# The indexer's keys and weights as one projection output, the keys' second copy by a transfer

## The reference, cut to what matters

```python
proj = h @ w_in                                   # (512, 1024) @ (1024, 3656)
(aq, ak, av, bq, bk, bv, cq, ck, cv, iq, ik, iw) = split(proj)
# iq: 8 heads x 64, ik: 64 (one key for all heads), iw: 8 weights
iw = iw * 8 ** -0.5
logits = einsum('bqhd,bkd->bqhk', iq, ik) * 64 ** -0.5
score = einsum('bqhk,bqh->bqk', relu(logits), iw)
score = where(key <= query, score, NEG)
_, idx = top_k(score, 128)
# attention of kind c over the keys idx only
```

## Time and profile before

| | |
|---|---|
| median of 3 runs | 2800.58 us (2800.39 to 2800.69) |
| the profiled execution, its own time | 2799.84 us |
| its span | 2797.8 us |
| TensorE busy | 2741.3 us, 98% |
| VectorE, ScalarE, POOL busy | 1171.8, 1029.3, 1110.1 us |
| mean granted TensorE clock | 0.995 of full speed |
| loads of packs | 456 of 512 KB, 3.6 us to landing (median) |

### The profile page before, as it was taken

One profiled execution on the slowest core, in us unless ns is written; L12 is line 12 of the kernel. 1 busy time (PEld: TensorE's weight loads), 2 busy tenths in 40 slices (PEclk: granted clock), 3 DMA queues, 4 the chain that ended last, 5 costly groups with the idle time before them and its releaser, 6 DMA issues.

```text
span 2797.8 us, 35422 instructions
## 1 busy us (share of the span) xinstructions
PE 2741.3 (98%) x12394; PEld 2174.0 (78%) x12394; DVE 1171.8 (42%) x1912; ACT 1029.3 (37%) x1571; POOL 1110.1 (40%) x473
## 2 busy tenths in 40 slices
PE   8999999999999999989989999999999999999998
PEld 6777777888887888846878888888888764788887
DVE  4886534654434224258873222122221266422212
ACT  4455533444333232352223222232222467422221
POOL 3334433444454444512214444544444410544443
PEclk9999999999999999999999999999999999999999
DMA  5333322333332333322203333333233310333332
GB/s 169 113 99 116 104 76 62 98 97 93 109 106 89 99 91 99 119 75 67 65 24 104 98 97 98 105 98 101 94 97 105 98 39 1 107 96 97 97 103 86
DMA packets 78106, 258.18 MB, mean 92 GB/s; under 512 B 8951, under 2 KB 14583, under 8 KB 77768
## 3 DMA queue, kind: packets, MB, share of 16 engines
q1 hardware_dynamic: 70848, 243.30, 28.4%
q10 hardware_dynamic: 7176, 13.78, 1.5%
HBM read 251.02 MB, written 6.03 MB: 92 GB/s over the span
## 4 chain that ended last, share of the span: by engine, by line
PE 93%; DVE 5%; ACT 1%; issue 1%; ACTq 0%; DVEq 0%
PE ps L765 27%; PE ps L767 27%; PE ps L766 27%; PE ps L1356 1%; PE ps L1338 1%; PE ps L1325 1%; PE ps L1329 1%; PE ps L985 1%; PE ps L1120 1%; PE ps L1052 1%; PE ps L1062 1%; PE ps L986 0%; PE ps L987 0%; PE ps L970 0%; PE ps L887 0%
## 5 line engine op out<-in xcount | busy, mean ns | idle before, releaser
L718 POOL TENSOR_TENSOR wlo<-raw,whi 128x1024 fp32r<-128x1024 f32 x449 | 1097.8, 2448 | 1640.4 <-ACT whi L1425 1615.6
L765 PE MATMUL ps<-lin_hi,whi 128*128 128x512 f32 x2208 | 867.8, 393 | 6.6 <-DVE waves_tmp L2445 6.6
L767 PE MATMUL ps<-lin_hi,wlo 128*128 128x512 f32 x2208 | 860.2, 390 | 0.0
L766 PE MATMUL ps<-lin_lo,whi 128*128 128x512 f32 x2208 | 860.2, 390 | 0.0
L1425 ACT ACTIVATE whi<-raw 128x1024 fp32r<-128x1024 f32 x452 | 473.3, 1053 | 513.8 <-PE ps L767 446.6
L765 PEld LDWEIGHTS ps<-lin_hi,whi 128*128 128x128 f32 x2208 | 415.1, 188 | 99.7 <-DVE waves_tmp L2445 7.4
L766 PEld LDWEIGHTS ps<-lin_lo,whi 128*128 128x128 f32 x2208 | 415.2, 188 | 88.1 <-issue 2.9
L767 PEld LDWEIGHTS ps<-lin_hi,wlo 128*128 128x128 f32 x2208 | 415.1, 188 | 87.0
L765 PE MATMUL ps<-act_hi,whi 128*128 128x512 f32 x858 | 334.0, 389 | 0.0
L767 PE MATMUL ps<-act_hi,wlo 128*128 128x512 f32 x858 | 333.8, 389 | 0.0
L766 PE MATMUL ps<-act_lo,whi 128*128 128x512 f32 x858 | 333.8, 389 | 0.0
(11 more groups left out here) (374 smaller groups left out, 2702.7 us busy)
## 6 DMA issues: line engine op xcount, KB each, us to landing
raw<-in_packs SPq DMA_DIRECT2D x456, 512.0 KB, 3.6
table<-bias_scratch ACTq DMA_DIRECT2D x12, 256.0 KB, 2.9
bias_scratch<-biasrow ACTq DMA_DIRECT2D x16, 160.0 KB
x<-in_x_t SPq DMA_DIRECT2D x4, 512.0 KB, 8.0
out_t<-x SPq DMA_DIRECT2D x16, 128.0 KB, 1.8
bias_scratch<-biasrow ACTq DMA_DIRECT2D x4, 320.0 KB
mem<-in_mem_t ACTq DMA_DIRECT2D x1, 1024.0 KB, 7.7
pool_count<-in_pool_count ACTq DMA_DIRECT2D x1, 1024.0 KB, 4.8
```

The source lines that it names most:

```text
L718: pool.tensor_tensor(wlo[:, n % 4, :], raw[:, n % 2, :], whi[:, n % 4, :].bitcast(F32), ALU.subtract).then_inc(low_split, 1)
L765: pe.matmul(target, wh, hi[:, k, :], start=(chunk0 + at == 0), stop=False)
L766: pe.matmul(target, wh, lo[:, k, :], start=False, stop=False)
L767: mm = pe.matmul(target, wl, hi[:, k, :], start=False, stop=(chunk0 + at == total - 1))
```

## The change

The keys and the weights are made by one output. Its pack is put together by the load: for each of the 8 chunks the first 64 columns of the keys' pack and the first 64 of the weights' pack, so that rows 0 to 63 of the output are the keys and rows 64 to 71 the weights. The second copy of the keys, for the logits of the other half of the rows, is made by a transfer within the on-chip memory, issued by ScalarE in slot 4, into the tile that held the weights; TensorE waits for it before the first index logits. The mixer has 29 outputs, and three padding packs. The keys' output is fourth, IQ + 3 fifth. The constants that place side work by slots are one less, except `BIAS_A_AT`; step 0 of ScalarE splits two packs, and TensorE passes two padding packs in it. The identity's transfer counts into the semaphore of the bias's inputs, which frees a semaphore for the copy.

```diff
-N_MIXER = 30
+MIXER_TILES = 30
+N_MIXER = MIXER_TILES - 1
+KEYS_AGAIN = IW
-MIX_ORDER = [IQ, IQ + 1, IQ + 2, IQ + 3, IK, IW] + [t + h for h in range(4) for t in (AQ, AK, AV)] + \
-    [...] + [30, 31]
+MIX_ORDER = [IQ, IQ + 1, IQ + 2, IK, IQ + 3] + [t + h for h in range(4) for t in (AQ, AK, AV)] + \
+    [...] + [30, 31, 31]
...
-BIAS_A_AT, BIAS_B_AT = 2, 6
-IDX_AT = 6
-A_FROM = 10
+BIAS_A_AT, BIAS_B_AT = 2, 5
+IDX_AT = 5
+A_FROM = 9
...
@@ sync, load
+            if n == behind(IK) - 1 and i is None:
+                sp.dma_start(raw[:, n % 2, :].rearrange("p (k s c) -> p k s c", k=DC, s=2),
+                             A["packs"][IK:IW + 1].rearrange("s p (k c) -> p k s c", c=P)[:, :, :, 0:64]).then_inc(raw_arrived[n % 2], 16)
+                return
@@ tensor, index_weights
-            pe.wait_ge(outs_done, behind(IW))
+            pe.wait_ge(outs_done, behind(IQ + 3))
...
-                mm = pe.transpose(ps[:, 2, t * 8:(t + 1) * 8], proj[0:8, IW, t * P:(t + 1) * P], ident[0:8, 0:8])
+                mm = pe.transpose(ps[:, 2, t * 8:(t + 1) * 8], proj[64:72, IK, t * P:(t + 1) * P], ident[64:72, 64:72])
@@ tensor, index_logits
                 pe.wait_ge(root_ready, 1)
+                pe.wait_ge(keys_copied, 16)
...
-                          proj[r:r + 64, IK, 0:(qt + 1) * P], start=True, stop=True).then_inc(idx_logits, 1)
+                          proj[r:r + 64, (IK, KEYS_AGAIN)[side], 0:(qt + 1) * P], start=True, stop=True).then_inc(idx_logits, 1)
@@ tensor, steps
-            if s < 2:
-                pe.wait_ge(low_split, N_MIXER + s + 1)
-                pe.wait_ge(packs_used, N_MIXER + s)
+            for n in ((29, 30), (31,))[s] if s < 2 else ():
+                pe.wait_ge(low_split, n + 1)
+                pe.wait_ge(packs_used, n)
                 pe.sem_inc(packs_used, 1)
@@ scalar, between
+            if n == behind(IK):
+                act.wait_ge(outs_done, behind(IK))
+                act.dma_start(proj[64:P, KEYS_AGAIN, :], proj[0:64, IK, :]).then_inc(keys_copied, 16)
@@ scalar, steps
+            if s == 0:
+                split_high(N_MIXER + AHEAD)
             if s < PAIR_STEPS + KV_FROM:
-                split_high(N_MIXER + AHEAD + s)
+                split_high(N_MIXER + AHEAD + 1 + s)
@@ vector, slots
-                              ALU.mult).then_inc(outs_done, 1 if n < N_MIXER - 1 else 3)
+                              ALU.mult).then_inc(outs_done, 1 if n < N_MIXER - 1 else 33 - N_MIXER)
```

More of the change, by code:

```diff
@@ L93 @@
 AQ, AK, BQ, BK, CQ, CK, IQ, IK, IW, AV, BV, CV = 0, 4, 8, 10, 12, 14, 16, 20, 21, 22, 26, 28
-N_MIXER = 30
-MIX_ORDER = [IQ, IQ + 1, IQ + 2, IQ + 3, IK, IW] + [t + h for h in range(4) for t in (AQ, AK, AV)] + \
-    [t + h for q, k, v in ((BQ, BK, BV), (CQ, CK, CV)) for h in range(2) for t in (q, k, v)] + [30, 31]
+MIXER_TILES = 30
+N_MIXER = MIXER_TILES - 1
+KEYS_AGAIN = IW
+MIX_ORDER = [IQ, IQ + 1, IQ + 2, IK, IQ + 3] + [t + h for h in range(4) for t in (AQ, AK, AV)] + \
+    [t + h for q, k, v in ((BQ, BK, BV), (CQ, CK, CV)) for h in range(2) for t in (q, k, v)] + [30, 31, 31]
 V_TILES = [AV, AV + 1, AV + 2, AV + 3, BV, BV + 1, CV, CV + 1]
@@ L115 @@
 APART = 8
-BIAS_A_AT, BIAS_B_AT = 2, 6
-IDX_AT = 6
-A_FROM = 10
+BIAS_A_AT, BIAS_B_AT = 2, 5
+IDX_AT = 5
+A_FROM = 9
 TURN_AT, PRODUCT_AT, SUM_AT, SUM_READ_AT, ROOT_AT, SCALE_AT = A_FROM + 2, A_FROM + 6, A_FROM + 7, A_FROM + 8, A_FROM + 9, A_FROM + 10
-V_AT = (12, 13, 15, 19, 23, 24, 28, STEPS_AT + 2)
-MEM_AT = 13
-TOP_FROM, TOP_TO = 8, N_MIXER - 1
+V_AT = (11, 12, 14, 18, 22, 23, 27, STEPS_AT + 2)
+MEM_AT = 12
+TOP_FROM, TOP_TO = 7, N_MIXER - 1
 def top_rounds(n):
@@ L261, in build_program @@
     put, m1 = region(big_at)
-    proj = put("proj", [P, N_MIXER, T])
+    proj = put("proj", [P, MIXER_TILES, T])
     o_hi_at = m1["at"]
@@ L443, in build_program @@
     cols_arrived = sem("cols_arrived")
-    ident_arrived = sem("ident_arrived")
+    keys_copied = sem("keys_copied")
     rel_arrived = sem("rel_arrived")
@@ L840, in bias_rows @@
         def bias_rows():
-            pe.wait_ge(rel_arrived, 16 * 2)
+            pe.wait_ge(rel_arrived, 16 * 3)
             pe.wait_ge(rel_apart, 1)
@@ L953, in _ @@
                 bias_rows()
-                pe.wait_ge(ident_arrived, 16)
             between(n)
@@ L1552, in _ @@
         act.dma_start(relb[:, :], A["rel_bias"]).then_inc(rel_arrived, 16)
-        act.dma_start(ident[:, :], A["ident"]).then_inc(ident_arrived, 16)
+        act.dma_start(ident[:, :], A["ident"]).then_inc(rel_arrived, 16)
         act.wait_ge(mask_cleared, 1)
@@ L2160, in _ @@
         order(dve.memset(relb_apart[:, :], 0.0))
-        dve.wait_ge(rel_arrived, 16 * 2)
+        dve.wait_ge(rel_arrived, 16 * 3)
         dve.tensor_scalar(relb_apart[:, ::APART], relb[:, :], 8.0, None, ALU.mult).then_inc(rel_apart, 1)
```

## The result

The changed kernel takes 2806.04 us (median; 2804.91 to 2808.3), the kernel before 2800.64 us on the same chip (2799.17 to 2805.08). The ratio is 1.0015 with a 95% interval of 1.0008 to 1.0022: slower by 0.15%, some 4.2 us, and within the 0.2% that was called no change. The time is outside the range on record, 2796.3 to 2804.5, and 4.1 us above the forecast of 2801.9. The profiled execution took 2805.23 us, its span 2803.1.

The account below looks back on a forecast made before the run. TensorE was taken as the bound, busy for 98% of the span. The terms -5.45 + 3.8 + 1.7 + 1.3 = +1.35 us gave 2801.2 for the profiled execution and 2801.9 us for the median; range 2796.3 to 2804.5, 8 in 10.

Parts of the forecast that it names:

- Term 2: Before the first index logits: TensorE waits for the keys' copy, held behind bias spreads until 51.0; +3.8 us.
- Term 3: Behind the wait for the keys: TensorE's clock falls to half for 3.4 us; +1.7 us.
- term 4: Pair stage: pack 34's load comes later, ScalarE's split delays the copies before TensorE's second turn; +1.3 us.
- Term 1: Mixer's projection: one output of 24 matmuls goes, side work moving forward costs nothing; -5.45 us.
- late bound: Keys' copy: its whole trip begins only at 50.4, so it lands at 53.3 and the wait is 6.1 us.
- like the first: Earlier trace, 1435.5 to 1439.3: TensorE nearly idle, then half clock from 1440.5 to 1443.8; the forecast wait likened to it.
- Term 5: Pack 3's load in 2048 pieces of 256 B: landed by 17.6, before POOL begins; 0 us.
- D: Keys' copy at its late bound, 53.3, and a second half-clock stretch: +2.3 and +1.7, 2805.9 us; chance 0.09.
- A: Keys' copy not held by the spreads, lands at 42; only terms 1 and 4 remain: -4.1 us, 2796.4; chance 0.15.
- B: Wait for keys comes, but clock not lowered or pair stage absorbs its gap: 2800.2 to 2800.6 us; chance 0.25.
- C: Pack 3's load in 256 B pieces lands at 43.9, TensorE 17.1 us late: +14.7, 2815.3 us; chance 0.04.

Follow-up runs that it names:

- Run 7: Changed kernel with pack 3 loaded as one plain pack in whole rows, instead of 2048 pieces of 256 B; 2806.62 us, ratio 1.0016.
- run 2: Changed kernel with pack 32's split ahead of step 0's exponentials on ScalarE instead of behind them; 2803.54 us, ratio 1.0007.
- Run 6: Changed kernel with five unread matmuls on TensorE between the weights' transposes and the first logits; 2804.7 us, ratio 1.0008.
- run 1: Changed kernel with the keys' copy issued by SyncE ahead of pack 8's load, not by ScalarE; 2797.34 us, ratio 0.9986.
- run 4: Changed kernel with the keys' copy still on ScalarE's queue but ahead of the third bias spread; 2798.82 us, ratio 0.9988.
- Run 5: Kernel before, with only pack 32's split moved from slot 29 to step 0, behind its exponentials; 2804.58 us, ratio 1.0008.
- run 3: Changed kernel with the copy issued by SyncE and pack 32's split ahead of step 0's exponentials; 2795.51 us, ratio 0.9975.
- run 9: The kernel of run 3 (copy on SyncE, pack 32's split first) measured once more; 2797.04 us, ratio 0.9976.
- run 10: Run 3's kernel with pack 34's split moved behind step 2's exponentials, its second measurement; 2797.17 us, ratio 0.9980.
- run 11: Changed kernel with the copy on SyncE and pack 34's split behind step 2's exponentials, pack 32's split left late; 2796.94 us, ratio 0.9980.

## Why the prediction was wrong

The place of every loss was right. Two sizes were not (terms 2 and 3), and in term 4 a second delay was put at nothing; all three on the same side.

**Term 1 (-5.45) was right:** -5.44. The slots behind it, whose packs all moved by one, gained and lost nothing: from the second logits to the first pair scores it is 166.42 us in the old profile and 166.40 in the new one. From the first product of the pair stage to the end of the mixer it is 63.93 and 63.92.

**Term 2 (+3.8) was 1.6 us too small: 5.4.** The chain of reasoning held: the spreads end at 50.4 by the forecast, at 51.4 in the trace, which is 50.4 plus the 0.93 of the late start. What failed is the line "0.3 us for its own 33 kB there, with a landing". Its own pieces took 1.0 us on the four engines, where the fourth spread comes onto them too, and the landing 1.0 more: 2.0 us where 0.6 stood for both, and 0.1 until the matmul. The neighbour with the whole trip of 2.9 us, used for the late bound only, was the better guide: here a landing cost 2.0 us of these 2.9 although the last pieces were the end of what stood ahead.

**Term 3 (+1.7) was 1.2 us too small: 2.9.** The step "a wait of 3.8 us ... is like the first" of the earlier trace rows did not fit the longer wait of 5.3 us: two stretches of half clock came, not one. Run 7 had a wait of 4.7 us and one stretch, run 2, with the changed kernel's copy and 5.3 us, again two. Run 6 shows that the idleness brings them. In the two profiles with two stretches the clock fell before the logits began (52.9 for 53.5, 52.2 for 53.1), in run 7 at about their start (53.0 for 52.9), so that part of the longer stretch passed with TensorE idle. What decides between one and two was not settled.

**Term 4 (+1.3) was 0.9 us too small: 2.2.** The forecast held for its mechanism and for the size of its step: ScalarE waits for pack 34 (3.55 us; forecast some 3), TensorE's second turn for ScalarE, and that turn comes 1.15 us later than before; forecast 1.3. What failed is "in the steps behind it I find no further wait": 0.88 us more are lost until the third turn, 0.68 of them a gap that waits for VectorE's probabilities. The gap at the second turn is only 0.70 because TensorE comes to it late itself, with its first memory pack at half clock (3.87 us from the first matmul of it to the last, where run 1 has 2.86). That half clock costs nothing of its own: the stage takes 24.57 to 24.63 us with it (changed kernel, runs 5 and 7) and 24.58 to 24.72 without it (runs 1, 4 and 6). Run 5 shows the whole sum with the late split alone.

**Term 5 (0) was right:** landing after 4.8 us, 1.5 more than the whole load of run 7, at 17.7 us; ScalarE comes to splitting packs 3 and 4 only at 21.52 and POOL to the remainders at 24.27, neither held by a load. The estimate by the Trainium skill ("DMA: Bandwidth & Descriptors", on why small descriptors are slow), 27% more for pieces of 256 B, was 1 us; the pair of landings here gives 45%.

**The sum.** 1.6 + 1.2 + 0.9, the start's 0.93, and -0.65 in the rest and in rounding make 3.98; the span's change was +5.3 where +1.35 was forecast. The start's part is chance of one execution. Without it the forecast and the three errors make 1.35 + 3.7 = 5.05, between the 4.2 us of the ratio and the 5.4 of the medians.

**The rivals.** D was nearest, 2805.9 for 2806.04, with both of its marks: a landing of 53.4 (its bound was 53.3) and a second stretch of half clock. It had a chance of 0.09, since it was built as two mishaps together; they are not independent, as the later copy makes the longer wait. That it meets the time to 0.1 us is in part luck: its landing bound of 53.3 is 0.8 too late once the late start is taken off (53.4 less 0.93 is 52.5), and it has nothing of the 0.9 that term 4 missed; the two cancel. A was wrong for this kernel. Run 1, where the other queue issues the copy, and some 2 us sooner, comes near its 2796.4, with no wait, though with a landing of 6.8 us and not 3. B was wrong, C was refuted by run 7.

## What to carry to other kernels

A transfer that is spread over all DMA engines is as late as its share on the busiest ones: place it by what stands ahead of it on those engines, not by its own size, and give it a whole trip of its own behind them. Price a wait of TensorE of this length with the half clock that follows it; here that was half of the wait again, and the cause for both is one late landing. Where TensorE waits for something else anyway, as in the pair stage, the half clock cost nothing. Where a change empties a slot, look at the loads that the buffer's turn sets off: a split one slot late cost 2.2 us two steps on, and one line's place in the order gave it back, though not in every execution.

## What was not expected of the hardware

One kernel's executions fall into groups some 3 to 4 us apart. The changed kernel of run 1 has 2796.0 to 2798.6 and then 2801.4 to 2801.6. The profiles of runs 1 and 3, which fell into a low and a high group, differ most in these windows, run 1 first:
```profile
1212.00:1219.00 7.00, 4.28 (x8) 1.99 (x8) 4.67 (x8) 6.99 (x11) 0.00 (x0) 0.51 0.34 132
1219.00:1226.00 7.00, 7.00 (x21) 2.73 (x20) 6.97 (x9) 6.43 (x13) 0.00 (x0) 1.00 0.01 2
```
```profile
1212.00:1219.00 7.00, 3.51 (x7) 1.94 (x8) 3.90 (x7) 6.97 (x12) 0.00 (x0) 0.50 0.47 157
1219.00:1226.00 7.00, 7.00 (x10) 2.42 (x9) 6.65 (x8) 6.48 (x12) 0.00 (x0) 0.54 0.01 2
```
The half clock ends near 1219 in the one and goes on to 1226 in the other, with the same program around it: 6.8 or 13.65 us, and 2.6 us more from there to the last matmul. Runs 5, 9, 10 and 11 have the long stretch as well, the other eight profiles the short one. Runs 2, 3, 6 and 7 also had 3.4 us of half clock near 283 to 292 us that the others had not, 1.5 us each. And ahead of the pair stage's first turn TensorE waits 1.97 to 2.01 us in every profile, with 3.4 us of half clock behind it in five of the thirteen (both kernels, runs 2, 5 and 7) and none in eight.

That such stretches make the groups is borne out by the mean granted clock of the executions that were not profiled. Of the 90 executions of the kernel before beside these runs, the 22 with 0.993 take 2804.3 us or more, the 63 with 0.995 or 0.996 take 2802.6 or less, and 5 with 0.994 lie between them. Why one execution gets the longer stretch stays open. Before such differences a single profile's span says little at this size; the sums above were therefore taken from stretch to stretch and not from spans.
